# A hybrid decoder layer whose value tiles start from an input laid out features-first

## What is computed

```python
h = rms_norm(x, norm1_g[l])
proj = jnp.einsum('bsd,dc->bsc', h, w_in[l])
q, k, v, xp, gates = ...            # 512, 512, 512, 512 and 2048 columns
a = diff_attention(rms_norm(q), rms_norm(k), v, lam)
merged = gates0 * (a @ w_up_attn) + gates1 * (pool_mixer(xp) @ w_up_pool)
x = x + merged @ w_o
x = x + square(relu(rms_norm(x, norm2_g) @ w_mlp_in)) @ w_mlp_out
```

## Time and profile before

| | us |
|---|---|
| median of three runs | 1250.93 |
| lowest, highest | 1250.3, 1252.01 |
| span of the profiled execution | 1249.3 |
| TensorE busy | 1240.8 |
| VectorE busy | 937.9 |
| ScalarE busy | 556.4 |
| GpSimd busy | 141.4 |

### The profile page before, as it was taken

One profiled execution on the slowest core, in us unless ns is written; L12 is line 12 of the kernel. 1 busy time (PEld: TensorE's weight loads), 2 busy tenths in 40 slices (PEclk: granted clock), 3 DMA queues, 4 the chain that ended last, 5 costly groups with the idle time before them and its releaser, 6 DMA issues.

```text
span 1249.3 us, 16209 instructions
## 1 busy us (share of the span) xinstructions
PE 1240.8 (99%) x5885; PEld 1022.0 (82%) x5885; DVE 937.9 (75%) x1316; ACT 556.4 (45%) x961; POOL 141.4 (11%) x198
## 2 busy tenths in 40 slices
PE   9999999999999999999999999999999999999999
PEld 6878888887788888888887888888888888888887
DVE  5547786778987778754688778778679988879764
ACT  5436665666553324322345545445445333333330
POOL 2113223223300040000000000000000000000035
PEclk9999999999999999999999999999999999999999
DMA  7100120103375457332213553453569644363223
GB/s 274 35 17 16 58 60 19 38 23 106 127 261 177 144 188 267 119 117 86 100 65 129 170 175 123 160 173 112 176 240 363 218 158 167 102 236 102 101 95 141
DMA packets 110354, 169.75 MB, mean 136 GB/s; under 512 B 5806, under 2 KB 55875, under 8 KB 110276
## 3 DMA queue, kind: packets, MB, share of 16 engines
q1 hardware_dynamic: 110274, 168.72, 39.5%
q10 hardware_dynamic: 2, 0.00, 0.0%
HBM read 118.37 MB, written 50.33 MB: 135 GB/s over the span
## 4 chain that ended last, share of the span: by engine, by line
PE 89%; DVE 5%; ACT 3%; issue 2%; DMA 1%; SPq 0%; POOL 0%; ACTq 0%; DVEq 0%
PE bank L2301 81%; PE bank L2443 2%; PE bank L2422 2%; PE bank L2381 1%; DVE slot_lo L1504 1%; DMA x_tile<-in_x 1%; DVE c L2201 1%; DVE pair_lo L2095 1%; PE bank L2372 1%; PE bank L2658 1%; DVE small L1587 1%; DMA gate_store<-out_tile 1%; PE bank L2319 0%; ACT slot_hi L1022 0%; ACT prob L1067 0%
## 5 line engine op out<-in xcount | busy, mean ns | idle before, releaser
L2301 PE MATMUL bank<-o_hi,s_lo 128*128 128x512 f32 (+1 forms) x452 | 175.0, 387 | 0.0
L2301 PE MATMUL bank<-o_hi,s_hi 128*128 128x512 f32 (+1 forms) x452 | 175.0, 387 | 0.0
L2201 DVE TENSOR_TENSOR c<-bank,c 128x512 f32<-128x512 f32 x112 | 75.7, 688 | 35.6 <-PE bank L2301 33.9
L2301 PE MATMUL bank<-featT_hi,pair_hi 128*128 128x512 f32 x256 | 99.9, 390 | 0.7 <-DVE c L2201 0.6
L2301 PE MATMUL bank<-o_lo,s_hi 128*128 128x512 f32 (+1 forms) x260 | 100.3, 386 | 0.0
L2301 PE MATMUL bank<-featT_lo,pair_hi 128*128 128x512 f32 x256 | 99.6, 389 | 0.0
L2301 PE MATMUL bank<-featT_hi,pair_lo 128*128 128x512 f32 x256 | 99.6, 389 | 0.0
L2301 PEld LDWEIGHTS bank<-o_hi,s_hi 128*128 128x128 f32 x452 | 84.9, 188 | 17.5
L2301 PEld LDWEIGHTS bank<-o_hi,s_lo 128*128 128x128 f32 x452 | 84.9, 188 | 17.2
L1472 ACT ACTIVATE s_hi<-s_raw 128x2048 fp32r<-128x2048 f32 x28 | 53.7, 1917 | 94.6 <-DMA s_raw<-u_store 94.6
L1448 ACT ACTIVATE c<-c 128x512 f32<-128x512 f32 x64 | 39.9, 624 | 118.8 <-DVE c L2201 118.8
(11 more groups left out here) (283 smaller groups left out, 3158.0 us busy)
## 6 DMA issues: line engine op xcount, KB each, us to landing
s_raw<-u_store SPq DMA_DIRECT2D x28, 1024.0 KB, 5.6
pair_raw<-in_w_mlp_in SPq DMA_DIRECT2D x16, 1024.0 KB, 5.9
u_store<-s_tile SPq DMA_DIRECT2D x64, 256.0 KB, 2.1
o_raw<-in_w_mlp_out SPq DMA_DIRECT2D x16, 1024.0 KB, 8.3
u_store<-u_tile SPq DMA_DIRECT2D x48, 256.0 KB, 2.4
gate_store<-out_tile SPq DMA_DIRECT2D x32, 256.0 KB, 2.6
gate_raw<-in_w_in SPq DMA_DIRECT2D x8, 1024.0 KB, 5.4
raw<-in_w_in SPq DMA_DIRECT2D x12, 512.0 KB, 4.8
```

The costliest lines, as they stand in the source:

```text
L2201: nc.vector.tensor_tensor(out[:], psum, other[:], ALU.add).then_inc(up_sum, 1)
L2301: mm = nc.tensor.matmul(out, a, b, start=start and i == 0, stop=stop and i == len(steps) - 1, skip_group_check=onto)
```

## The change

The input x is given to the kernel a second time, features-first: `x_cols[t]` is the row tile t with its features on the partitions, 128 x (8 blocks x 128 tokens). The norm's gain is given as `g1_cols`, a value per partition and block, and the small vectors as `vec_cols`, all laid out ahead of the launch. So nothing is transposed: the gain is one value per partition and block, and the row factor varies along the free axis.

Tiles 0 to 2 (`t < PLAIN`) go into their value products without the row factor: VectorE multiplies by the gain (`scale_plain`), ScalarE and VectorE split (`plain_hi_part`, `plain_lo_part`), and the factor is applied when the value tile is taken out of PSUM, where tokens are on the partitions (`v_hi_part`, `v_lo_part` with `x_rstd`). Tiles 0 and 1 are made together in `v_first`, weight block by weight block, each block now loaded and split by itself (256 KB, 512 columns).

Tiles 3 to 7, and later 0 to 2 for the other projections, are normalised: GpSimd multiplies tiles 3 to 7 by the gain (`scale_rows`, a 128x1024 instruction each); VectorE makes a 128x128 diagonal of the row factors, hi and lo (`make_diagonal`); TensorE multiplies ones by it, which spreads the factors over all partitions (`spread`, two 128-column products); VectorE multiplies the tile by that, out of PSUM (`scale_columns`), ScalarE and VectorE split it (`h_hi_part`, `h_lo_part`). The order of normalising is 3, 4, 0, 5, 1, 6, 2, 7. The row tiles are still loaded and squared, in that order, for the row factor alone. Four value banks are used instead of two. TensorE leads with eight products of ones instead of four. Several semaphores are shared between the start and later stages, with higher counts there.

```diff
+        PLAIN = 3
+        NORM_ORDER = (3, 4, 0, 5, 1, 6, 2, 7)
+        nth_normed = NORM_ORDER.index
...
+            return (4, 5, 2, 3)[t % 4]
...
+            def load_xT(t):
+                if t > 5:
+                    sp.wait_ge(h_split, nth_normed(t - 3) + 1)
+                sp.dma_start(xT[xT_place(t)][:].rearrange("p k n -> p (k n)"), x_cols[t]).then_inc(xT_in[xT_place(t)], 16)
+            def load_x(n):
+                if n > 1:
+                    sp.wait_ge(x_squared, n - 1)
+                sp.dma_start(x_tile[n % 2][:], x_rows[NORM_ORDER[n]]).then_inc(x_in[n % 2], 16)
+            def load_v_w(k):
+                sp.dma_start(raw[k // 2][:, HALVES[k % 2]], w_in_v[:, k, V0:V0 + HEADS * P]).then_inc(
+                    (even_in, raw_in)[k % 2][k // 2], 16)
...
+            load_xT_half(0, 0)
             load_v_w(0)
             load_v_w(1)
+            load_xT_half(1, 0)
             load_v_w(2)
+            load_v_w(3)
+            load_xT_half(0, 1)
+            load_xT_half(1, 1)
+            for k in range(4, KD):
+                load_v_w(k)
+            load_xT(2)
+            load_x(0)
+            load_xT(3)
             load_x(1)
-            load_v_w(3)
+            load_xT(4)
             load_x(2)
...
+            load_xT(5)
+            load_x(3)
+            load_qk(0, 0)
+            load_x(4)
+            load_qk(0, 1)
+            load_xT(6)
+            load_x(5)
+            load_qk(0, 2)
+            load_x(6)
+            load_xT(7)
+            load_qk(0, 3)
+            load_x(7)
+            sp.dma_start(col[:], vec_cols).then_inc(vec_in, 16)
...
+            def scale_rows(t):
+                xT_loaded(pool, t)
+                if t == PLAIN:
+                    pool.wait_ge(vec_in, 16)
+                now = xT[xT_place(t)]
+                pool.tensor_tensor(now[:], now[:], g1_col[:].unsqueeze(2).to_broadcast([P, KD, P]),
+                                   ALU.mult).then_inc(pool_xg_ready, 1)
...
+            for n, t in enumerate(NORM_ORDER):
+                if t >= PLAIN:
+                    scale_rows(t)
+                x_inverse(n, t, x_squared, x_mean, x_inv)
...
+            def h_hi_part(t):
+                act.wait_ge(h_ready, nth_normed(t) + 1)
+                if t < PLAIN:
+                    act.wait_ge(v_full, t + 1)
+                nc.scalar.activation(featT[0][:, :, columns(t)], xT[xT_place(t)][:], ACT.Copy).then_inc(h_hi, 1)
...
+            plain_hi_part(0, TOP)
             v_w_hi(0)
-            x_hi(0, (0,))
             v_w_hi(1)
-            x_hi(0, (1,))
-            g1_copy(0)
-            x_square(1)
-            g1_copy(1)
+            plain_hi_part(1, TOP)
             v_w_hi(2)
             v_w_hi(3)
-            x_hi(1)
+            plain_hi_part(0, BOTTOM)
+            plain_hi_part(1, BOTTOM)
+            for k in range(4, KD):
+                v_w_hi(k)
+            plain_hi_part(2, ALL_K)
+            x_square(0)
+            x_square(1)
+            h_hi_part(3)
             x_square(2)
...
+            h_hi_part(4)
+            x_square(3)
+            v_hi_part(0)
+            h_hi_part(0)
+            x_square(4)
+            h_hi_part(5)
+            qk_weights_hi(0, 0)
+            x_square(5)
+            v_hi_part(1)
+            h_hi_part(1)
+            qk_weights_hi(0, 1)
+            x_square(6)
+            h_hi_part(6)
+            v_hi_part(2)
+            x_square(7)
+            h_hi_part(2)
...
+            def scale_plain(t, ks):
+                b = ks.start // 4
+                if t < 2:
+                    dve.wait_ge((xT_first, xT_in)[b][t], 16)
+                else:
+                    xT_loaded(dve, t)
+                n = ks.stop - ks.start
+                nc.vector.tensor_tensor(xT[t][:, ks, :], xT[t][:, ks, :], g1_col[:, ks].unsqueeze(2).to_broadcast([P, n, P]),
+                                        ALU.mult).then_inc(xg_ready, 1)
+            def plain_lo_part(t, ks):
+                dve.wait_ge(xg_ready, plain_number(t, ks.start // 4))
+                dve.wait_ge(plain_hi, plain_number(t, ks.start // 4))
+                nc.vector.tensor_tensor(featT[1][:, ks, columns(t)], xT[t][:, ks, :], featT[0][:, ks, columns(t)],
+                                        ALU.subtract).then_inc(plain_split, 1)
+            def make_diagonal(t):
+                n = nth_normed(t)
+                hi, lo = diag[n % 2]
+                if n == 0:
+                    dve.wait_ge(const_ready, 1)
+                dve.wait_ge(x_inv, n + 1)
+                wait(dve, spread_full, n - 1)
+                nc.vector.tensor_scalar(hi[:], ident[:], x_rstd[:, t:t + 1], None, ALU.mult).then_inc(diag_ready, 1)
+                dve.wait_ge(diag_ready, 2 * n + 1)
+                nc.vector.scalar_tensor_tensor(lo[:], ident[:], x_rstd[:, t:t + 1], hi[:], ALU.mult,
+                                               ALU.subtract).then_inc(diag_ready, 1)
...
+            def scale_columns(t):
+                n = nth_normed(t)
+                dve.wait_ge(spread_full, n + 1)
+                if t >= PLAIN:
+                    dve.wait_ge(pool_xg_ready, t - PLAIN + 1)
+                else:
+                    dve.wait_ge(plain_split, 5)
+                now = xT[xT_place(t)]
+                nc.vector.tensor_tensor(now[:], now[:], bank[:, spread_bank(t), 0:P].unsqueeze(1).to_broadcast([P, KD, P]),
+                                        ALU.mult).then_inc(h_ready, 1)
+            def h_lo_part(t):
+                n = nth_normed(t)
+                dve.wait_ge(h_ready, n + 1)
+                dve.wait_ge(h_hi, n + 1)
+                nc.vector.tensor_tensor(featT[1][:, :, columns(t)], xT[xT_place(t)][:], featT[0][:, :, columns(t)],
+                                        ALU.subtract).then_inc(h_split, 1)
...
+            make_diagonal(3)
+            scale_columns(3)
+            make_diagonal(4)
+            h_lo_part(3)
+            scale_columns(4)
+            make_diagonal(0)
+            h_lo_part(4)
+            v_lo_part(0)
+            scale_columns(0)
+            make_diagonal(5)
+            h_lo_part(0)
+            scale_columns(5)
+            make_diagonal(1)
+            h_lo_part(5)
+            qk_weights_lo(0)
+            scale_columns(1)
+            v_lo_part(1)
+            make_diagonal(6)
+            h_lo_part(1)
+            qk_weights_lo(1)
+            scale_columns(6)
+            make_diagonal(2)
+            h_lo_part(6)
+            v_lo_part(2)
+            scale_columns(2)
+            make_diagonal(7)
+            h_lo_part(2)
+            v_lo_part(3)
+            qk_weights_lo(2)
+            qk_weights_lo(3)
+            v_lo_part(4)
+            scale_columns(7)
+            h_lo_part(7)
...
+            def spread(t):
+                n = nth_normed(t)
+                wait(pe, h_ready, n - 1)
+                pe.wait_ge(diag_ready, 2 * n + 2)
+                for i in range(2):
+                    mm = nc.tensor.matmul(bank[:, spread_bank(t), 0:P], ones[:, 0:P].bitcast(F32R), diag[n % 2][i][:],
+                                          start=i == 0, stop=i == 1)
+                mm.then_inc(spread_full, 1)
+            def v_project(t, spreads=()):
+                if t < PLAIN:
+                    pe.wait_ge(plain_hi, plain_number(t, 0))
+                else:
+                    pe.wait_ge(h_hi, nth_normed(t) + 1)
+                wait(pe, v_ready, t - 3)
+                for k in range(KD):
+                    for i, (a, b) in enumerate(((0, 0), (0, 1), (1, 0))):
+                        if k == 0 and i == 2:
+                            if t < PLAIN:
+                                pe.wait_ge(plain_split, plain_number(t, 0))
+                            else:
+                                pe.wait_ge(h_split, nth_normed(t) + 1)
+                        mm = nc.tensor.matmul(bank[:, v_bank(t), :], featT[a][:, k, columns(t)], v_w[b][:, k, :],
+                                              start=k == 0 and i == 0, stop=k == KD - 1 and i == 2)
+                    for after, other in spreads:
+                        if k == after:
+                            spread(other)
+                mm.then_inc(v_full, 1)
...
+            def v_first(k):
+                b = k // 4
+                pe.wait_ge((even_hi, w_hi)[k % 2], k // 2 + 1)
+                for t in range(2):
+                    for i in range(2):
+                        if k % 4 == 0:
+                            pe.wait_ge((plain_hi, plain_split)[i], plain_number(t, b))
+                        nc.tensor.matmul(bank[:, v_bank(t), :], featT[i][:, k, columns(t)], v_w[0][:, k, :],
+                                         start=k == 0 and i == 0, stop=False)
+                pe.wait_ge((even_ready, w_ready)[k % 2], k // 2 + 1)
+                for t in range(2):
+                    mm = nc.tensor.matmul(bank[:, v_bank(t), :], featT[0][:, k, columns(t)], v_w[1][:, k, :],
```

(17 more changed lines are left out.)

352 lines of the change are left out of this document (134 added, 218 removed).

## The result

The changed kernel takes 1257.19 us, the median of four runs (1255.2 to 1258.01), against 1250.64 before in the same sitting: a ratio of 1.0047, 95% interval 1.0034 to 1.006. It is slower by 6.5, and the forecast was 1256.8. So the number is right. Several of its parts are not, and their errors nearly cancel, as the experiments and the part behind them show.

The account below looks back on a forecast made before the run. TensorE's own queue was taken to bound the kernel (busy 99% of the span). The rewritten stretch was to end at 79.3 instead of 73.4, so 1249.3 + 5.9 + 1.6 = 1256.8 us; range 1248 to 1261.

Parts of the forecast that it names:

- The place: From the start to the first query-key transposes: the only stretch that changes; nothing behind the first attention tile moves over 0.5.
- The start: Value tiles 0 and 1: `v_first` ends near 21.3, against value tile 2 starting at 25.80 before, a gain of 4.5.
- the rise: TensorE at the start: step from the 1.2 to the 2.4 GHz level, product starts 0.42 then 0.24 apart, at 13.1.
- TensorE's own work: TensorE from 21.3 to the stretch's end: 43.8 of products plus 1.8 for eight spreads, 45.6, to 66.9 without waits.
- The waits: TensorE after `v_first`: named waits add 11.7, sign 10 to 13; wrong if under 6; 0.1 per restart after long ones.
- the price of the multiplication: GpSimd's multiplication of a tile by the gain: 2.4 each, with 1.9 and 2.6 as ends.
- walk: Queues followed link by link through the stretch: end at 79.3 against 73.4, +5.9; with GpSimd at 1.9, 78.2, +4.8.
- rival 4: TensorE's clock level rises late or falls again in waits of 2.3 to 2.6: +7.3, 1258.2, to 1261; chance 0.10.
- The holds: GpSimd's multiplications hold VectorE's diagonals near 40 and 51, a whole instruction at a time; two holds of 2.1.
- Rival 2: GpSimd and VectorE do not hold each other: two holds of 2.1 go, end 76.3, +2.9, 1253.8; chance 0.10.
- Rival 1: VectorE keeps ahead of TensorE, every wait from 21.3 on goes: end 66.9, -6.5, 1244.4; chance 0.13.
- Rival 3: Level rises early, `v_first` ends at 16.5 to 20, but tile 3's chain limits: 1254.9 with GpSimd at 1.9; chance 0.08.

Follow-up runs that it names:

- e1: The changed kernel run once more, unaltered; 1257.36 us, ratio 1.0043 to the kernel before.
- e2: The changed kernel with GpSimd multiplying one element of each block by the gain instead of 1024 columns; 1256.64 us.
- e9: The changed kernel with GpSimd's multiplication by the gain written as two of 512 columns instead of one of 1024; 1256.95 us.
- e4: The changed kernel without the row factor for the columns: no diagonals, spreads or multiplication of the columns by it; 1243.53 us, ratio 0.9936.
- e10: The changed kernel's operations in a rearranged written order on its engines and loads, meant to remove GpSimd's holds; 1246.01 us, ratio 0.9966 to the kernel before.
- e5: The changed kernel with eight extra products on ones just ahead of the first query-key tile's wait for the third weight quarter; 1254.88 us.
- e11: The same as e10 with six more products on ones in TensorE's idle time at the start; 1246.67 us, ratio 0.9962 to the kernel before.
- e3: The changed kernel with six more products on ones in TensorE's idle time at the start; 1255.24 us.

## Why the prediction was right, and where it was not

**The place.** Right. The change of the mark is the change of the span to 0.1, and nothing behind the first attention tile moved by more than that.

**The start.** Forecast 21.3 with the rise at 13.1. Measured 21.89 in the chain, with a rise where it had been (starts of products, 0.41 and then 0.24 apart):

```profile
12.46 0.58 PE L2644 MATMUL bank<-v_w_hi,featT_hi 128*128 128x512 f32 x1
12.87 0.40 PE L2644 MATMUL bank<-v_w_hi,featT_lo 128*128 128x512 f32 x1
13.11 0.63 PE L2648 MATMUL bank<-v_w_lo,featT_hi 128*128 128x512 f32 x2
```

The second x block was late: VectorE has it at 7.96 and not at 6.9. I had read its landing from two larger loads; it also varies, 7.2 to 8.0 in the profiles of kernels with the same first loads. Its wait ended at 9.37 and not at 8.3, so two or three fewer products ran before the rise. Lead 3.9, forecast 4.5.

That the rise came at 13.1 again is luck. It is a second one:

```profile
6.06 0.40 PE L2644 MATMUL bank<-v_w_hi,featT_lo 128*128 128x512 f32 x1
9.37 0.76 PE L2644 MATMUL bank<-v_w_hi,featT_hi 128*128 128x512 f32 x1 [2.90 <-ACT featT_hi L1088]
```

```profile
10.00:12.00 2.00, 1.96 (x5) 1.49 (x5) 2.00 (x5) 0.41 (x2) 0.00 (x0) 0.50 1.07 407
```

The product at 6.06 took 0.40, what products take at the fast level, behind the eight leading ones; then came the wait of 2.90, and the granted clock was 0.50 from 9.4 to 12.8. My forecast had no early rise and no fall here. In e1 the product at the same place took 0.63 and the one rise came at 13.5. Over the profiles of all kernels with this start the last rise lies between 12.1 (e2) and 14.5 (e9).

**TensorE's own work.** Forecast 45.6. e4 has 43.54 for the products, and a spread is 0.17 to 0.18 in the chains of the changed kernel and e10, so 1.4 for eight: 44.9. Of a restart I took 0.1 after each long wait, 0.7 in all; the twelve products behind the wait of 2.20 took 3.06 where twelve take 2.72, so 0.34. From 21.89 to 77.69, the end of the last product, are 55.8: 44.9, 8.4 of waits, and 2.5 left over for seven restarts.

**The waits.** All seven came, in order. Forecast 11.7 with 0.2 for spread(3), measured 8.4; that is under the 10 to 13 that I had given as a sign, and over the 6 below which I would have been wrong:

| | forecast | measured |
|---|---|---|
| tile 3's subtraction | 0.7 | 0.5 |
| value tile 0 | 0.8 | 0.5 |
| spread(5) | 1.0 | 0.8 |
| spread(1) | 2.6 | 1.6 |
| value tile 1 | 1.7 | 1.5 |
| spread(2) | 2.3 | 1.3 |
| third weight quarter | 2.4 | 2.2 |

Most of the miss is the two spreads behind a GpSimd hold. The term that was mis-sized is the price of the multiplication: I took 2.4, twice the row of an in-place 512-column addition of two full tensors. The one that runs reads one full tensor and one broadcast value per block, and took 1.90, as the addition of a tensor to its own shift did. It may be nearer to that row in what it reads; I had picked the other for being in place. My own walk at 1.90 gave +4.8, and the stretch came out at +4.1, in place of the +5.9 of my sum.

**The clock.** Here the forecast left out what its own rival 4 named. I made forecast and fall exclude each other: either the waits add 5.9, or the clock falls as well and it is more. What happens is the smaller sum of waits, +4, with the fall behind the last of them in more than half of the executions if their length is the sign of it (three spans of four in the first sitting, three of five in e1), 2.0 of median by e5. 1249.3 + 4.1 + 1.6 is 1255.0, which is what the profiled execution took (1255.2); 1257 is that plus the fall. The number was right by luck, by errors of opposite sign. In the stretch it had 3.3 too much of waits and 0.7 too much of TensorE's own work, against 1.8 too little of restarts and 0.6 too little of start; that leaves 1.6 of the 1.8 too much (the rest lies in where the two ends were read), and about 2 of clock was missing.

**The holds.** That they come and where was right (diagonals of 1.58 that end with GpSimd's instruction, near 39 and near 49). Their size was not: 1.3 each over the 0.28 of a free one, where the walk had about 2.1, since the multiplication is 0.5 shorter and begins 0.4 ahead of the diagonal. The step that was held has one tensor input and a value per partition, and not two tensors as in the rows that I argued from. The same section of the Trainium skill, "SBUF — State Buffer", "Who interferes with whom", says that such an operation of VectorE can take the shared pair too, in its two-port modes; the trace agrees that it was held, 1.58 under GpSimd and 0.28 without; in which mode it ran no row shows. Rival 2 (no hold) priced them at 3; e2 gives 1.2 of wait at most, since the next waits take up the rest.

**Rivals.** Rival 1 (VectorE keeps ahead) gave 66.9 and 1244.4. It was false for the order as written and nearly true for the operations: e10 and e11 have them all and reach the mark at 68.1 and 67.2. My argument for it, 4.1 of VectorE work to a turn of 5.7, was sound as to amount. Rival 3 had an earlier rise bring little (0.8 with GpSimd at 1.9, nothing at 2.4), as the chain was to start with tile 3's block; e3 shows that 1.8 of 2.0 passes through to the third weight quarter.
